# Merge stages of a two-block transformer kernel: raw weights and the first twelve inputs loaded in place, low parts split anew between VectorE and GpSimd

## What is computed

```python
# end of the first block (the second has the same two products, another norm behind them)
g = jax.nn.sigmoid(gates + merge_bias)
y = g[:, :, 0] * (a @ w_branch_a) + g[:, :, 1] * (b @ w_branch_b)   # 2048 x 1024
x = x + y @ w_out
# second block: y from w_proj_a_2 and w_proj_b_2, then x + gate * rms(y @ w_out_2)
```

## Time and profile before

| | |
|---|---|
| three executions | 3564.94, 3572.80, 3568.74 us (median 3568.74) |
| profiled execution | 3571.06 us; its span 3569.3 us, mean granted TensorE clock 0.939 |
| merge part of out1 | first DMA issue at 1661.90, last merge matmul about 1887 us |
| merge part of out2 | first DMA issue at 3158.65, last merge matmul about 3383 us |
| DMA, whole span | 458.20 MB, mean 128 GB/s |

### The profile page before, as it was taken

One profiled execution on the slowest core, in us unless ns is written; L12 is line 12 of the kernel. 1 busy time (PEld: TensorE's weight loads), 2 busy tenths in 40 slices (PEclk: granted clock), 3 DMA queues, 4 the chain that ended last, 5 costly groups with the idle time before them and its releaser, 6 DMA issues. The chain is left out here.

```text
span 3569.3 us, 43493 instructions
## 1 busy us (share of the span) xinstructions
PE 3204.4 (90%) x15878; PEld 2629.3 (74%) x15878; DVE 1759.3 (49%) x3726; ACT 1562.5 (44%) x2453; POOL 1171.6 (33%) x790
## 2 busy tenths in 40 slices
PE   3996999889995999967989959997999999978999
PEld 3995788667874677755768848876888888866787
DVE  3775789979994666522332135661322132123432
ACT  2453679756973777721111023333444344421111
POOL 2541012100223899922222223332222222222222
PEclk9997999999997999976999969998999999989999
DMA  4665433343334211045553244546444644345622
GB/s 112 178 197 193 133 106 95 116 152 95 105 93 130 66 58 38 28 171 188 153 129 120 95 137 144 166 131 226 127 132 136 219 127 132 122 117 136 156 83 95
DMA packets 434159, 458.20 MB, mean 128 GB/s; under 512 B 30897, under 2 KB 318129, under 8 KB 432305
## 3 DMA queue, kind: packets, MB, share of 16 engines
q1 hardware_dynamic: 433968, 455.72, 41.6%
HBM read 289.70 MB, written 165.94 MB: 128 GB/s over the span
## 5 line engine op out<-in xcount | busy, mean ns | idle before, releaser
L1426 POOL TENSOR_SCALAR a_prob<-a_prob,a_inv 128x128 f32<-128x128 f32 (+15 forms) x128 | 384.2, 3024 | 83.3 <-DVE a_inv L1467 83.1
L2346 PE MATMUL p_pr<-p_hT,p_w_hi 128*128 128x512 f32 x896 | 351.6, 392 | 18.1 <-DMA p_hT<-s_hT 18.1
L1258 PE MATMUL p_pr<-p_hT,p_w_hi 128*128 128x512 f32 x896 | 355.4, 397 | 13.3 <-POOL p_w_lo L1041 9.5
L1259 PE MATMUL p_pr<-p_hT,p_w_hi 128*128 128x512 f32 x896 | 353.2, 394 | 0.0
L1260 PE MATMUL p_pr<-p_hT,p_w_lo 128*128 128x512 f32 x896 | 352.7, 394 | 0.0
L2347 PE MATMUL p_pr<-p_hT,p_w_hi 128*128 128x512 f32 x896 | 349.9, 391 | 0.0
L2348 PE MATMUL p_pr<-p_hT,p_w_lo 128*128 128x512 f32 x896 | 349.3, 390 | 0.0
L758 PE MATMUL t_pj_ps<-t_w_hi,t_hT_slot 128*128 128x356 f32 (+2 forms) x768 | 274.1, 357 | 40.8 <-POOL t_w_lo L474 26.6
L1041 POOL TENSOR_TENSOR p_w_lo<-p_w_raw,p_w_hi 128x256 fp32r<-128x256 f32 x144 | 108.0, 783 | 616.1 <-DVE p_level L1178 401.9
L1081 ACT ACTIVATE p_relu<-p_isc,p_level 128x2048 int8<-128x2048 f32 (+5 forms) x192 | 276.4, 1441 | 20.9 <-DVE p_level L1178 16.9
L1953 PE MATMUL o_b_ps<-o_in_hi,o_w_hi 128*128 128x512 f32 x512 | 214.9, 420 | 74.3 <-POOL o_in_lo L1848 45.4
(11 more groups left out here) (272 smaller groups left out, 7095.3 us busy)
## 6 DMA issues: line engine op xcount, KB each, us to landing
p_w_raw<-in_w_in SPq DMA_DIRECT2D x112, 512.0 KB, 4.3
s_hT<-t_hT_slot SPq DMA_DIRECT2D x32, 1024.0 KB, 5.7
p_hT<-s_hT SPq DMA_DIRECT2D x64, 512.0 KB, 10.0
s_gT<-p_o_sb SPq DMA_DIRECT2D x128, 256.0 KB, 4.9
o_gates<-s_gT SPq DMA_DIRECT2D x64, 512.0 KB, 5.1
s_qT<-t_qT_slot SPq DMA_DIRECT2D x32, 512.0 KB, 2.7
s_zuT<-p_o_sb SPq DMA_DIRECT2D x64, 256.0 KB, 4.9
pl_wada<-in_w_ada SPq DMA_DIRECT2D x6, 2048.0 KB, 14.1
```

The costliest lines, as they stand in the source:

```text
L1258: nc.tensor.matmul(pr[n % NPR][:], wh, hi, start=(k == 0), stop=False)
L1259: nc.tensor.matmul(pr[n % NPR][:], wh, lo, start=False, stop=False)
L1426: nc.gpsimd.tensor_scalar(prob[:, slot, 0:n], prob[:, slot, 0:n], inv[:, slot:slot + 1], None, ALU.mult).then_inc(normed, 1)
L2346: nc.tensor.matmul(pr[n % NPR][:], wh, hi, start=(k == 0), stop=False)
```

## The change

Both merge parts are changed, in one function:

- `load_split_weights` and its two raw places go away. `w_raw`, all 8 pieces, lies where `wo_raw` lay, that is in the bytes of `w_lo`. Pieces are loaded without any wait, and the low part of a piece overwrites its raw.
- `in_raw`, 12 places, lies in the bytes of `in_lo`. The first twelve inputs are loaded into it without any wait, each on a semaphore of its own, and their low parts overwrite them. Inputs 12 to 31 go through `src` as before; input 12 is issued at u = 2 (it was at u = 4), and so on: u+10 in place of u+8.
- VectorE makes the low parts of all weight pieces and of inputs 0, 2, 4 and 6 (`ON_DVE = range(0, KD, 2)`); GpSimd those of all other inputs and of no merge weight.
- SP's order: piece 0, inputs 0 to 7, piece 1, gates 0, piece 2, gates 1, pieces 3 to 7, inputs 8 to 11, then the loop over units.
- `yT` is laid out by token tile: 16 tiles of 8 x 128, so the sum of line 1917 writes four runs of 128, and a tile is read as one run of 1024.

```diff
-    yT = sb("yT", [P, KD, SEQ], F32)
+    yT = sb("yT", [P, T, KD, P], F32)
...
+        w_raw = c.alloc(shared, tag)[0]("w_raw", [P, KD, D], F32)
     w_lo = sb("w_lo", [P, KD, D], F32R)
...
+        in_raw = c.alloc(shared, tag)[0]("in_raw", [P, RING, BANK], F32)
     in_lo = sb("in_lo", [P, RING, BANK], F32R)
...
+    def raw(x):
+        return in_raw[:, x] if x < RING else src[:, x % 2]
...
             def load_src(x):
-                if x >= 2:
-                    sp.wait_ge(lo_done, x - 1)
+                if x >= RING + 2:
+                    wait_low(sp, x - 2)
...
-            load_src(0)
-            load_src(1)
-            sync(sp, range(0, 2))
-            for x in range(2, KD):
+            load_weights(0)
+            for x in range(KD):
                 load_src(x)
+            load_weights(1)
             load_gates(0)
+            load_weights(2)
             load_gates(1)
-            sync(sp, range(2, KD))
+            for n in range(3, KD):
+                load_weights(n)
+            for x in range(KD, RING):
+                load_src(x)
             for u in range(UNITS_ALL):
                 if u + 2 < UNITS_ALL:
                     load_gates(u + 2)
-                if u + KD < UNITS_ALL:
-                    load_src(u + KD)
+                if RING <= u + KD + 2 < UNITS_ALL:
+                    load_src(u + KD + 2)
...
@@ gpsimd
             for x in range(GROUPS * KD):
-                if x == 2:
-                    gpsimd(pool, range(0, 2))
-                if x == KD:
-                    gpsimd(pool, range(2, KD))
+                if x not in ON_DVE:
...
@@ scalar
+            high_weights(0)
             for x in range(GROUPS * KD):
-                if x == 2:
-                    scalar(act, range(0, 2))
                 if x == KD:
-                    scalar(act, range(2, KD))
+                    for n in range(1, KD):
+                        high_weights(n)
...
@@ vector
-            vector(dve, range(KD))
+            low_merge(0)
+            for x in ON_DVE:
+                dve.wait_ge(hi_done, x + 1)
+                nc.vector.tensor_tensor(in_lo[:, x], raw(x), f32(in_hi[:, x]), ALU.subtract).then_inc(lo_done[0], 1)
+            for n in range(1, KD):
+                low_merge(n)
             for u in range(UNITS_ALL):
...
-                nc.vector.tensor_tensor(yT[:, dc, tg * BANK:(tg + 1) * BANK], gates[:, u % 2, 0], gates[:, u % 2, 1], ALU.add
+                nc.vector.tensor_tensor(yT[:, tg * GROUPS:(tg + 1) * GROUPS, dc], both[0], both[1], ALU.add
```

More of the change, by code:

```diff
@@ L1686, in _ @@
                 ada_product(pe, n)
[L1689 to L1724, removed]
 def phase_output(c, stack, second):
@@ L1747, in phase_output @@
     with ExitStack() as shared:
-        x_in = c.alloc(shared, "r2" if second else "r1")[0]("x_in", [P, 2, D], F32)
+        x_in = c.alloc(shared, tag)[0]("x_in", [P, 2, D], F32)
     in_hi = sb("in_hi", [P, RING, BANK], F32R)
+    with ExitStack() as shared:
+        in_raw = c.alloc(shared, tag)[0]("in_raw", [P, RING, BANK], F32)
     in_lo = sb("in_lo", [P, RING, BANK], F32R)
@@ L1758, in phase_output @@
     x_out = gates[:].rearrange("p s b n -> p s (b n)")
[L1760 to L1764, removed]
+    w_loaded, w_hi_done, w_lo_done = [sem(f"w_loaded{n}") for n in range(KD)], sem("w_hi_done"), sem("w_lo_done")
+    raw_loaded = [sem(f"raw_loaded{x}") for x in range(RING)]
     src_loaded, g_loaded = [sem("s_even"), sem("s_odd")], [sem("g_even"), sem("g_odd")]
-    hi_done, lo_done, multiplied, weighed, summed = (sem("hi_done"), sem("lo_done"), sem("multiplied"),
+    hi_done, lo_done, multiplied, weighed, summed = (sem("hi_done"), [sem("lo_dve"), sem("lo_pool")], sem("multiplied"),
                                                      sem("weighed"), sem("summed"))
@@ L1772, in phase_output, with part, wait_low @@
     squared, meaned, powered, scaled = sem("squared"), sem("meaned"), sem("powered"), sem("scaled")
-    def wo_part(w, k):
+    ON_DVE = range(0, KD, 2)
+    def part(w, k):
         return w[:, :, k * P:(k + 1) * P]
     def tile(t):
-        return yT[:, :, t * P:(t + 1) * P]
+        return yT[:, t]
+    def wait_low(eng, x):
+        if x in ON_DVE:
+            eng.wait_ge(lo_done[0], ON_DVE.index(x) + 1)
+        else:
+            eng.wait_ge(lo_done[1], x + 1 - sum(y in ON_DVE for y in range(x)))
+    def raw(x):
+        return in_raw[:, x] if x < RING else src[:, x % 2]
     def o_ps(t):
@@ L1788, in load_src, with load_weights @@
                 cols = slice(tg * BANK, (tg + 1) * BANK)
-                if x >= 2:
-                    sp.wait_ge(lo_done, x - 1)
-                part = c.aT[k] if k < KB else c.bT[k - KB]
-                sp.dma_start(src[:, x % 2], part[:, cols]).then_inc(src_loaded[x % 2], 16)
+                if x >= RING + 2:
+                    wait_low(sp, x - 2)
+                branch = c.aT[k] if k < KB else c.bT[k - KB]
+                sp.dma_start(raw(x), branch[:, cols]).then_inc(raw_loaded[x] if x < RING else src_loaded[x % 2], 16)
+            def load_weights(n):
+                for half, w in enumerate((wa, wb)):
+                    sp.dma_start(part(w_raw, n)[:, half * KB:(half + 1) * KB],
+                                 w[0, :, n * P:(n + 1) * P].rearrange("(k p) n -> p k n", p=P)).then_inc(w_loaded[n], 16)
             def load_gates(u):
@@ L1889, in _ @@
                 act.wait_ge(wo_loaded[k], 16)
-                nc.scalar.activation(wo_part(w_hi, k), wo_part(wo_raw, k), ACT.Copy).then_inc(wo_hi_done, 1)
+                nc.scalar.activation(part(w_hi, k), part(w_raw, k), ACT.Copy).then_inc(wo_hi_done, 1)
             act.wait_ge(summed, UNITS_ALL)
@@ L1916, in _ @@
                 dve.wait_ge(multiplied, u + 1)
-                nc.vector.tensor_tensor(yT[:, dc, tg * BANK:(tg + 1) * BANK], gates[:, u % 2, 0], gates[:, u % 2, 1], ALU.add
+                both = [gates[:, u % 2, j].rearrange("p (t n) -> p t n", n=P) for j in range(2)]
+                nc.vector.tensor_tensor(yT[:, tg * GROUPS:(tg + 1) * GROUPS, dc], both[0], both[1], ALU.add
                                         ).then_inc(summed, 1)
@@ L1944, in _ @@
                 if tg == 0:
-                    ready(pe, dc)
+                    pe.wait_ge(w_lo_done, dc + 1)
                 if u >= 4:
@@ L1950, in _ @@
                     if dc == 0:
-                        pe.wait_ge(lo_done, x + 1)
+                        wait_low(pe, x)
                     first, final = k % KB == 0, k % KB == KB - 1
@@ L1964, in _ @@
                 for j in range(2):
-                    o, part = b_ps[t % NO][:, j], slice(j * KB, (j + 1) * KB)
+                    o, cols = b_ps[t % NO][:, j], slice(j * KB, (j + 1) * KB)
                     for k in range(KD):
```

31 lines of the change are left out of this document (19 added, 12 removed).

## The result

The changed kernel takes 3543.78 us (median of 4 runs, 3543.16 to 3546.45), the kernel before 3566.99 (4 runs on the same footing): a ratio of 0.9934, interval 0.9917 to 0.9951. The forecast was 3543. The profiled execution took 3543.16 us and shows a span of 3541.2.

The account below looks back on a forecast made before the run. The merge matmuls idled 74.3 us, mostly behind GpSimd's low parts, at openings and token-group crossings; 11.4 + 12.15 + 2.8 + 1.2 = 27.6 us off the profiled 3571.06 gave 3543, range 3534 to 3561.

Parts of the forecast that it names:

- the opening's term: First issue to unit 4 in each merge stage: unit 4 at 34.0 us, 11.4 us earlier in out2, 12.15 in out1.
- 1 us for what is left of the low clock: Opening, units 1 to 3: 1 us added to their end at 33.1, giving unit 4 at 34.0.
- gates 0, piece 2, gates 1 and piece 3 are 2.1 MB at 227: Opening loads: at 227 GB/s these land by 22.4 us, so pieces 2 and 3 come in time.
- the offset of 2.6: Opening loads: 2.6 us added once to transfer times, from 1.57 MB landed 7.8 us after the first issue.
- rival 2: Opening loads at the best rate, 383 GB/s: piece 7 by 22, unit 4 at 33, 3541 us; chance 0.10.
- The window of 383: Profile window with the best load rate seen, 383 GB/s, which the prediction said moves packets of 2 KB.
- So nothing is charged, and the cover would have to shrink by 14 us to make it cost: Crossings: unit 7's multiply some 8 us late costs nothing, since PE needs it only at unit 11, 22 us on.
- The 13.52 us of before: Out2's first crossing in the kernel before; forecast to fall to 10.69, 2.8 us less.
- Rival 4: Crossings: VectorE, late through unit 7's gates, delays SP's loads; all six at 13.5 cost 12.8 us, 3560; chance 0.07.
- Rivals 1 and 3: Opening: loads at 227 GB/s, 3553 us, chance 0.17; unit 0's multiply in VectorE's queue behind piece 7, 3579, chance 0.04.
- rival 3: Opening: unit 0's multiply waits in VectorE's queue behind piece 7, landing at 47.9; 8 us lost, 3579; chance 0.04.
- VectorE's 7.6 us ahead of unit 0: Opening: VectorE's added low parts, 4 x 1.22 + 4 x 0.69 us, lie in waits for DMA and cost nothing.

Follow-up runs that it names:

- the repeats: The changed kernel run again unaltered, against the kernel before: 3543.79 us, ratio 0.9936, and once more 3542.8 us, ratio 0.993.
- four places, old order: Changed kernel with inputs from 12 on through four raw places instead of two and issued at u+8: 3530.12 us, ratio 0.9898 to the kernel before.
- the four places: Changed kernel with inputs from 12 on through four raw places, issued at u+10 as in the change: 3499.36 us, ratio 0.9816 to the kernel before.

## Why the prediction was right, and where its terms were off

- **The opening of out1 and out2** was the gain, as the prediction had it, and its mechanism was right: PE starts at 7.1 and 7.6 us (forecast 7.5), the inputs' last low part is through at 14.1 and 14.7 (15.1), piece 1's at 15.3 and 15.8 (16.5), and PE's own pace decides unit 4.
- **Where the opening's term was off.** It was 23.6 and measured 27.6: unit 4 came at 31.8 and 32.3, not 34.0. Piece 1's low part was through 1.2 and 0.7 us earlier, and the "1 us for what is left of the low clock" wasn't spent, since the clock rose at 12.3 and 11.9 us, before unit 1. These are nearly the whole 4.0.
- **A rate that was off and cost nothing.** The step "gates 0, piece 2, gates 1 and piece 3 are 2.1 MB at 227" carried a low rate over from a window in which only two raw places were open. Measured: 317 to 319 GB/s; 7.34 MB by 26.1 us, less the offset of 2.6, is a mean of 312. Piece 7 landed at 26.7 and 26.1, not 29.5. Since PE's pace decided, this entered only the slack, 1.6 and 2.6 us where the forecast had 0.8. Unit 4 came even before the 33 of rival 2, but piece 7 not by its 22.
- **Rival 2's page.** The windows with weights ran at 296 to 319 GB/s with the share at 1.01 to 1.06, beside 361 in the window that also had inputs, with rows of 2 KB. At 27 ns a packet of 512 bytes is 303 GB/s on 16 engines, at 84 to 87 ns a packet of 2 KB 377 to 390. The window of 383 isn't all packets of 2 KB, as the prediction has it: over a third of its bytes came in packets of 512. The Trainium skill, "DMA: Bandwidth & Descriptors", section "Specifications", calls 512 bytes enough for line rate; the rows show the engines full and still 12 to 18% below the window of 361, so the trace bears it out only in part.
- **The crossings: the step that failed** is "So nothing is charged, and the cover would have to shrink by 14 us to make it cost". I asked who waits for unit 7's multiply (nobody, and that held: it came 8.5 us late and no wait of PE stands behind line 1907 there) and not what the gates of units 7 and 8 share the DMA with, nor what the late sum does to GpSimd's last subtraction. The first crossings were to fall to 10.69; they came to 11.60 and 11.66, and the others rose by 0.3 to 1.1 us. Putting the order back gave 0.8 us a crossing. The 13.52 us of before, 2.8 of the 4.0, stand in one execution; no second trace shows whether it is the rule. Rival 4 had the right place at over three times the price: against the forecast it charged 12.8 + 4 us, and the crossings came 4.8 above it.
- **Rivals 1 and 3** (slow loads, VectorE's queue) didn't come about. The run in which the weights wait shows that rival 3's mechanism was well placed, some 2.5 us of piece 7 away.
- **Costed at nothing** were `yT`'s layout (held: 3540.7 with the old one) and VectorE's 7.6 us ahead of unit 0 (held: no wait at unit 4). The semaphores have no row of their own; outside the openings and the crossings the two stages took 0.8 us less than before, so no cost of them shows.
- **The signs.** PE's waits for low parts in the opening fell to 0.4 us and less, as named (in one of the repeats one of them took 1.4). Two signs did not come: unit 4 was to start at 33 to 36 us and started at 31.8 and 32.3; the crossings were to take 10.5 to 11 us and five of six took more. The DMA share to 30 us was 0.91 and 0.89.
- The two errors, −4.0 and +4.8, cancelled to 0.8 us, and the rest of the stages gave these 0.8 back. The sum's accuracy is luck, and so is the choice of a profiled execution 4.1 us above the median as its base; either error alone would still have lain in the range.

## What to carry to other kernels

When a load is moved earlier in a queue that issues in order, ask what it now stops in front of and what then moves beside it; both the change and its undoing paid for one blocked load at each crossing, and the full gain came only when the load had a place of its own and could be issued early. A rate read from a window in which the DMA share was 0.86 is in part a measure of how much was queued; read it from one with a share near 1. And a wait between token groups is worth more than its own idle time here, since PE's clock also fell with it.

## What the runs showed of the hardware that I had not expected

- **Waits at the crossings cost twice.** With waits of 3.9 and 2.3 us out2's group 1 had a granted clock of 0.94, so part of it was spent at the lower of TensorE's two levels, 1.2 GHz. With the old order and waits of 1.3 to 2.8 us it was 0.93 all the same. With one long wait (four places, old order) it was 0.93 in out1 (3.5 and 4.0 us) and 0.97 in out2 (4.2 us). With none over 0.7 us it was 1.00, and the same matmuls took 2.3 us less, a third of what the four places brought per group.
- **GpSimd and VectorE take turns.** In the opening two subtractions of VectorE took 2.93 us (0.69 each alone) beside three of GpSimd in 4.68 (1.28 each); one after the other, these five would take 5.2. At a crossing they took 1.77 and 1.72. The Trainium skill, "SBUF — State Buffer", section "SBUF: two separate sides", has two-input VectorE operations and GpSimd's exclude each other; the rows agree but for half a microsecond in those five, though even so moving half of the low parts to VectorE was worth 4 us a stage.
- **Open.** The kernel with SP's old order is 6 to 11 us faster by its medians and only 4 to 5 by its two stages. What the rest is, no run tells.
